# Attention sweep of a hybrid trunk: the value products are divided between the transposes of two heads

## The chip, the cores and the metric

The kernel runs on one NeuronCore of a Trainium2 chip. The metric is the device time of one execution in microseconds (us); the median of three runs of the kernel before is 3368.22 us. The kernel is written by hand in five instruction streams, one for each engine: TensorE (PE, with its weight loads as PEld), VectorE (DVE), ScalarE (ACT), GpSimd (POOL) and SyncE (SP), which wait for one another by semaphores.

## The reference, cut to what matters

One layer over 2048 tokens of width 1024: RMS norm with adaLN, one input projection split in eight, an HGRN2 group of 8 heads, a stick-breaking attention group of 16 heads of size 64, gates, an output projection, a residual and a final norm, all in float32. The change lies in the attention alone:

```python
# one layer: rms norm, adaLN, u = h @ w_in, split in 8; an HGRN2 head group and this one, then w_out
def stick_breaking_attention(q, k, v):     # (1, 2048, 16 heads, 64)
    for nb in range(seq // QBLOCK):        # 128 queries at a time
        z = jnp.einsum('bhtd,bhsd->bhts', qh[:, :, t0:t1], kh[:, :, :t1]) * scale
        mask = jnp.arange(t1)[None, :] < (t0 + jnp.arange(QBLOCK))[:, None]
        log_keep = jnp.where(mask, jax.nn.log_sigmoid(-z), 0.0)
        rc = lax.cumsum(log_keep, axis=3, reverse=True)
        after = jnp.concatenate([rc[..., 1:], jnp.zeros_like(rc[..., :1])], axis=-1)
        w = jnp.where(mask, jnp.exp(jax.nn.log_sigmoid(z) + after), 0.0)
        outs.append(jnp.einsum('bhts,bhsd->bhtd', w, vh[:, :, :t1]))
```

## The kernel before, in words

The functions run one after the other: conditioning and input projection, HGRN2 heads, `stick` (the attention), `output`. Only `stick` is touched.

**The mathematics of `stick`.** With keep = sigmoid(-z), the weights w are differences of the running product `run` of keep from the right. By summation by parts, the output of a query is a sum over keys of (1 - run) times the difference of two neighbouring rows of v. POOL makes these differences (`delta`, tile `ad`, L937). So there are four steps for a piece of a query block: scores z on PE (L966, L969, L971), sigmoid on ACT (L1050, tile `akeep`), running product on DVE (L1086, a tensor_tensor_scan, tile `run`), and then a transposition of each 128x128 block on PE (L983, into `t_ps`), 1 - run on ACT from PSUM (L1058, tile `wt`) and the value product on PE (L1003, into `o_ps`).

**Tiling.** Heads are taken in pairs (e = 0 and 1), and there are 8 pairs. For a pair, the 16 query blocks of 128 are cut into 24 pieces by keys, numbered 0 to 23. Pieces 0 to 7 are query blocks 0 to 7, of 128, 256, ... 1024 keys. Pieces 8 to 15 are blocks 8 to 11, two pieces each: 640, 768, 896 or 1024 keys, and then the first 512. Pieces 16 to 23 are blocks 12 to 15: again 640 to 1024 keys, and then the first 1024. A piece of over 512 keys has two parts (`part_list`), since `t_ps` is two PSUM tiles of 512 columns, used in turn. There are 16 such pieces for a pair of heads (4 to 8, 10, 12, 14 and 16 to 23), and 8 pieces of one part.

**Order of the work.** The order is written out by hand. In step n (of 8 x 24 = 192) PE does `scores` of piece n for both heads, `transposes` of piece n-2 for both heads, `weighted` (the value product) of piece n-3 and, after the last piece of four query blocks, `rows` (L1013: four transpositions of the output back into rows):

```python
if there(n, last):
    scores(i, n)
if there(n - LAG_T, last):
    transposes(i, n - LAG_T)
if there(n - LAG_AV, last):
    weighted(i, n - LAG_AV)
```

ACT goes in the order: output copy of a group (L1038) and squares (L1043) where there are any, the sigmoids of piece n (both heads), the copies `wt` of piece n-2 (head 0, head 1, part after part). DVE does the two scans of piece n. `transposes` waits for the scan of its head (`run_ready`), and from the third part on for the copy of two parts ago (`wt_ready`, because `t_ps` has two tiles). So the first part of head 1 of a two-part piece waits until ACT has copied the first part of head 0. `weighted` waits for the copies of its piece, made one step earlier; in it, each 128 keys are two matmuls of 64 columns, one for each head, in the two halves of the array.

**The tile `run`** has a buffer of 2049 columns for each head and for even and odd query blocks. A row lies at the right end of its buffer, and the last column holds 1, the start of the product. The scan that begins a query block therefore waits until the transpositions of the block two before it are done (`free`).

The 48 steps of two pairs of heads are the body of a hardware loop, which begins at step 7 (`sweep`).

Of the kernel before, what the change touches and what calls it, by code (L numbers as in the profile page):

```python
# [26 lines left out]
P = 128  # L27
D = 1024
SEQ = 2048
KD = D // P  # L30
TB = SEQ // P
# [5 lines left out]
SD = 64  # L37
# [724 lines left out]
def stick(nc, io, keep, scr, o_scr):  # L762
# [15 lines left out]
    NP = len(pieces)  # L778
    PP = 2 * NP
    parts = [[(lo + a, min(512, width - a)) for a in range(0, width, 512)] for _, lo, width in pieces]  # L780
    before = [sum(len(x) for x in parts[:n]) for n in range(NP)]
    NS = sum(len(x) for x in parts)
    group_end = [max(n for n in range(NP) if pieces[n][0] // 4 == g) for g in range(4)]
    half_end = max(n for n in range(NP) if pieces[n][0] < TB // 2)
    SCALE = float(SD) ** -0.5
    NH2 = SH // 2
    with ExitStack() as stack:
        m = Mem(nc, stack)
        q = m.sb("aq", [P, 2, 2, SEQ], F32R)
        k = m.sb("ak", [P, 2, 2, SEQ], F32R)  # L790
        val = m.sb("av", [P, TB, 2 * SD])
        prev = m.sb("ap", [P, TB, 2 * SD])
        delta = m.sb("ad", [P, 2, TB, 2 * SD])
        gat = m.sb("ag", [P, 2, TB, 2 * SD])
        keepf = m.sb("akeep", [P, 2, 2, D])
        run = m.sb("run", [P, 2, 2, SEQ + 1])
        wt = m.sb("wt", [P, 8, 512])
        ot = m.sb("aot", [P, 512])
        og = m.sb("aog", [P, TB, 2 * SD])
# [1 line left out]
        unit_b = m.sb("unit_b", [P, P], BF16)  # L801
        never_b = m.sb("never_b", [P, P], BF16)
        never = m.sb("never", [P, P])
        z_ps = [m.ps(f"z_ps{e}", [P, D]) for e in range(2)]
        t_ps = [m.ps(f"t_ps{a}", [P, 512]) for a in range(2)]
        o_ps = m.ps("o_ps", [P, 512])
# [7 lines left out]
        ones_set = m.sem("ones_set")  # L814
# [16 lines left out]
        def at(n):  # L831

            return (n // NP % 2,) + pieces[n % NP]

        def part_list(n, e):

            base = n // NP * (2 * NS) + 2 * before[n % NP] + e * len(parts[n % NP])
            return [(base + a,) + x for a, x in enumerate(parts[n % NP])]

        def last_part(n, e):  # L840

            return part_list(n, e)[-1][0]

        def group(n):

# [12 lines left out]
        def there(n, last):  # L858
            return 0 <= n and not (last and n >= PP)

        with nc.Block() as block:
# [83 lines left out]
            @block.tensor  # L945
            def _(pe):
                nc.tensor.sem_inc(r_ready, 1)
                pe.wait_ge(ones_set, 3)

                def scores(i, n):  # L950
                    b, qb, lo, width = at(n)
                    if n % NP == 0:
                        pe.wait_ge(k_in[b], i * 64 + 64 * (n // PP + 1))
                        pe.wait_ge(q_in[0], i * 256 + 128 * (n // NP + 1))
                    if n % NP == half_end + 1:
                        pe.wait_ge(q_in[1], i * 256 + 128 * (n // NP + 1))
                    for e in range(2):
                        pe.wait_ge(keep_ready, i * (2 * PP) + (2 * n + e + 1))
                        for a in range(0, width, 512):
                            wd = min(512, width - a)  # L960
                            diag = lo + a + wd == (qb + 1) * P
                            q_hi = q[:, e, 0, qb * P:(qb + 1) * P]
                            q_lo = q[:, e, 1, qb * P:(qb + 1) * P]
                            kk = k[:, b, e, lo + a:lo + a + wd]
                            zz = z_ps[e][:, a:a + wd]
                            nc.tensor.matmul(zz, q_hi, kk, start=True, stop=False)  # L966
                            if diag:

                                nc.tensor.matmul(z_ps[e][:, a + wd - P:a + wd], unit_b[:, :], never_b[:, :],  # L969
                                                 start=False, stop=False, skip_group_check=True)  # L970
                            mm = nc.tensor.matmul(zz, q_lo, kk, start=False, stop=True)  # L971
                        mm.then_inc(z_ready, 1)

                def transposes(i, n):
                    b, qb, lo, width = at(n)
                    for e in range(2):
                        pe.wait_ge(run_ready, i * (2 * PP) + (2 * n + e + 1))
                        src = run[:, e, qb % 2, SEQ - (qb + 1) * P:]
                        for a, key, wd in part_list(n, e):
                            if a >= 2:  # L980
                                pe.wait_ge(wt_ready, i * (4 * NS) + (a - 1))
                            for j in range(wd // P):
                                mm = nc.tensor.transpose(t_ps[a % 2][:, j * P:(j + 1) * P], src[:, key + j * P:key + (j + 1) * P],  # L983
                                                         keep["ident"][:, :])
                            mm.then_inc(t_ready, 1)

                def weighted(i, n):
                    b, qb, lo, width = at(n)
                    diag = lo + width == (qb + 1) * P
                    if diag and qb % 4 == 0:  # L990

                        pe.wait_ge(ot_ready, i * 8 + (4 * (n // NP) + qb // 4 + 1))
                    if n % NP == 0:
                        pe.wait_ge(delta_ready, i * 2 + (n // NP + 1))
                    lists = [part_list(n, e) for e in range(2)]
                    cols = slice((qb % 4) * P, (qb % 4 + 1) * P)
                    for c in range(len(lists[0])):
                        pe.wait_ge(wt_ready, i * (4 * NS) + (lists[1][c][0] + 1))
                        key, wd = lists[0][c][1:]
                        for j in range(wd // P):  # L1000
                            for e in range(2):
                                a = lists[e][c][0]
                                mm = nc.tensor.matmul(o_ps[e * SD:(e + 1) * SD, cols], delta[:, b, key // P + j, e * SD:(e + 1) * SD],  # L1003
                                                      wt[:, a % 8, j * P:(j + 1) * P], start=(diag and key == lo and j == 0),
                                                      stop=(lo == 0 and key + (j + 1) * P == width))
                    mm.then_inc(av_ready, 1)

                def rows(i, n):
                    g = group(n)
                    pe.wait_ge(ot_ready, i * 8 + (g + 2))  # L1010
                    pe.wait_ge(og_ready, i * 8 + (g + 1))
                    for j in range(4):
                        mm = nc.tensor.transpose(r_ps[:, j * P:(j + 1) * P], ot[:, j * P:(j + 1) * P], keep["ident"][:, :])  # L1013
                    mm.then_inc(r_ready, 1)

                def step(i, n, last):
                    if there(n, last):
                        scores(i, n)
                    if there(n - LAG_T, last):
                        transposes(i, n - LAG_T)  # L1020
                    if there(n - LAG_AV, last):
                        weighted(i, n - LAG_AV)
                    if there(n - LAG_R, last) and group(n - LAG_R) is not None:
                        rows(i, n - LAG_R)

                sweep(nc.tensor, step)
# [37 lines left out]
            def _(dve):  # L1064
                nc.vector.sem_inc(red_ready, 1)
                nc.vector.sem_inc(og_ready, 1)
                nc.vector.memset(run[:, :, :, SEQ:SEQ + 1], 1.0).then_inc(ones_set, 1)
                dve.wait_ge(never_in, 16)
                nc.vector.tensor_copy(never_b[:, :], never[:, :]).then_inc(ones_set, 1)
                nc.vector.tensor_copy(unit_b[:, :], keep["ident"][:, :]).then_inc(ones_set, 1)  # L1070
                dve.wait_ge(ones_set, 3)

                def step(i, n, last):
                    if there(n, last):
                        b, qb, lo, width = at(n)
                        diag = lo + width == (qb + 1) * P
                        at0 = SEQ - (qb + 1) * P + lo
                        for e in range(2):
                            dve.wait_ge(keep_ready, i * (2 * PP) + (2 * n + e + 3))
                            if diag and (qb >= 2 or n >= NP):  # L1080

                                free = max(x for x in range(n) if at(x)[1] == (qb - 2) % TB)
                                dve.wait_ge(t_ready, i * (4 * NS) + (last_part(free, e) + 1))
                            if not diag:
                                dve.wait_ge(run_ready, i * (2 * PP) + (2 * (n - 1) + e + 1))
                            nc.vector.tensor_tensor_scan(run[:, e, qb % 2, at0:at0 + width][:, ::-1], keepf[:, e, n % 2, 0:width][:, ::-1],  # L1086
                                                         keepf[:, e, n % 2, 0:width], run[:, e, qb % 2, at0 + width:at0 + width + 1],
                                                         ALU.mult, ALU.bypass).then_inc(run_ready, 1)
                    n2 = n - LAG_OG
                    if there(n2, last) and group(n2) is not None:  # L1090
# [362 lines left out]
```

## Time and profile before

| | us |
|---|---|
| median of 3 runs (range) | 3368.22 (3367.56 to 3371.39) |
| the profiled execution's own time | 3368.85 |
| its span, first to last instruction | 3367.1 |
| PE busy in the span | 3097.2 |
| DVE busy | 1517.6 |
| ACT busy | 973.4 |
| POOL busy | 491.8 |
| mean granted clock of TensorE, share of full | 0.979 |

The profile comes from one execution. A matmul's duration in it runs until its result is out, so matmuls overlap and a PE that shows as busy need not be at its peak; what counts for PE is the distance from one start to the next. In brackets behind a row of the timeline stands the idle time of that engine before the row, and what ended it. "issue" is idle time in which the engine waited for nothing that the profile shows.

### The profile page before, as it was taken

The page shows a single profiled execution, that of the slowest core. Times are in us where ns is not written, and L with a number is a line of the kernel's source. Part 1 is how long each engine was busy: PE and PEld are TensorE (multiplying, and loading weights), DVE is VectorE, ACT ScalarE, POOL GpSimd, SP SyncE. Part 2 cuts the span into 40 slices and gives each one's busy share as a digit, 9 for nine tenths or more (in the row PEclk, how much of TensorE's full clock was granted, in tenths as well). Part 3 has the DMA queues.
Part 4 walks back from the last instruction along what each step waited for, and adds up shares of the span by engine and source line. Part 5 has one row for each costly group of instructions (what it writes and reads, how often), then busy time and mean ns, then how long its engine had stood idle before and what let it go on. Part 6 is the DMA issues. An engine that isn't in the chain of part 4 may idle for free. (4 is left out here: it accounts for less than half of the span.)

```text
span 3367.1 us, 56899 instructions
## 1 busy us (share of the span) xinstructions
PE 3097.2 (92%) x22432; PEld 2721.8 (81%) x22432; DVE 1517.6 (45%) x1652; ACT 973.4 (29%) x1749; POOL 491.8 (15%) x218
## 2 busy tenths in 40 slices
PE   6899999999999999997888859989889998879998
PEld 5788888889999999997888837767767777758887
DVE  5212221111112211225878846866767777654343
ACT  4111111111110111100111136666666666631111
POOL 3211111111111111103545610000000000000000
PEclk9999999999999999998999979999999999989999
DMA  6123334443222122215443192352352351053221
GB/s 271 60 72 99 115 119 123 119 124 100 72 69 72 58 70 72 69 59 195 134 131 112 29 224 51 77 127 51 76 127 52 76 126 39 1 181 118 82 100 38
DMA packets 217944, 327.14 MB, mean 97 GB/s; under 512 B 11680, under 2 KB 159520, under 8 KB 204960
## 3 DMA queue, kind: packets, MB, share of 16 engines
q1 hardware_dynamic: 217296, 324.08, 32.3%
q8 instruction: 114, 1.87, 0.2%
q14 instruction: 70, 0.57, 0.1%
q10 hardware_dynamic: 464, 0.63, 0.1%
HBM read 207.22 MB, written 117.44 MB: 96 GB/s over the span
## 5 line engine op out<-in xcount | busy, mean ns | idle before, releaser
L1086 DVE TENSOR_TENSOR_SCAN run<-akeep,run 128x1024 f32<-128x1024 f32 (+7 forms) x384 | 667.7, 1780 | 286.8 <-ACT akeep L1050 189.1
L983 PE MATMUL t_ps<-ident,run 128*128 128x128 f32 x2176 | 300.8, 278 | 89.5 <-ACT wt L1058 89.5
L1050 ACT ACTIVATE akeep<-z_ps 128x1024 f32<-128x1024 f32 (+7 forms) x384 | 290.9, 776 | 274.4 <-PE z_ps L971 270.1
L983 PEld LDWEIGHTS t_ps<-ident,run 128*128 128x128 f32 x2176 | 243.7, 141 | 134.2 <-ACT wt L1058 87.8
L1058 ACT ACTIVATE wt<-t_ps 128x512 f32<-128x512 f32 (+3 forms) x640 | 306.5, 534 | 55.5 <-PE t_ps L983 54.9
L966 PE MATMUL z_ps<-ak,aq 128*128 128x512 f32 (+3 forms) x640 | 254.4, 397 | 39.9 <-DMA aq<-s_qlo 33.9
L370 PE MATMUL u_ps<-w_hi,h_lo 128*128 128x256 f32 x2048 | 287.5, 283 | 0.0
L370 PE MATMUL u_ps<-w_lo,h_hi 128*128 128x256 f32 x2048 | 287.5, 283 | 0.0
L370 PE MATMUL u_ps<-w_hi,h_hi 128*128 128x256 f32 x2048 | 287.5, 283 | 0.0
L1003 PE MATMUL o_ps<-wt,ad 128*64 128x128 f32 x4352 | 280.5, 277 | 5.6 <-issue 5.6
L643 PE MATMUL hps<-hq,hk 128*128 128x128 f32 x1792 | 219.9, 286 | 50.0 <-DVE hq L733 13.3
L1003 PEld LDWEIGHTS o_ps<-wt,ad 128*64 128x64 f32 x4352 | 234.1, 137 | 37.8 <-issue 37.5
L370 PEld LDWEIGHTS u_ps<-w_hi,h_hi 128*128 128x128 f32 x2048 | 264.3, 192 | 0.1
L370 PEld LDWEIGHTS u_ps<-w_lo,h_hi 128*128 128x128 f32 x2048 | 264.2, 192 | 0.0
L370 PEld LDWEIGHTS u_ps<-w_hi,h_lo 128*128 128x128 f32 x2048 | 264.2, 192 | 0.0
L361 PE MATMUL u_ps<-h_hi,w_hi 128*128 128x512 f32 x1024 | 254.7, 391 | 5.9 <-DVE w_lo L413 5.9
L643 PEld LDWEIGHTS hps<-hq,hk 128*128 128x128 f32 x1792 | 215.1, 201 | 54.6 <-issue 52.4
L361 PE MATMUL u_ps<-h_lo,w_hi 128*128 128x512 f32 x1024 | 253.1, 389 | 0.0
L361 PE MATMUL u_ps<-h_hi,w_lo 128*128 128x512 f32 x1024 | 252.9, 389 | 0.0
L971 PE MATMUL z_ps<-ak,aq 128*128 128x512 f32 (+3 forms) x640 | 252.6, 399 | 0.0
L361 PEld LDWEIGHTS u_ps<-h_hi,w_hi 128*128 128x128 f32 x1024 | 193.2, 189 | 46.5 <-issue 6.3
L340 POOL CAST w_hi<-w_raw 128x2048 fp32r<-128x2048 f32 x31 | 58.8, 1895 | 1163.5 <-DMA w_raw<-in_w_in 1163.5
(140 smaller groups left out, 3621.6 us busy)
## 6 DMA issues: line engine op xcount, KB each, us to landing
w_raw<-in_w_in SPq DMA_DIRECT2D x32, 1024.0 KB, 5.6
aq<-s_qhi SPq DMA_DIRECT2D x64, 256.0 KB, 6.4
aq<-s_qlo SPq DMA_DIRECT2D x64, 256.0 KB, 6.9
o<-s_o SPq DMA_DIRECT2D x16, 1024.0 KB, 6.1
ada<-in_w_ada SPq DMA_DIRECT2D x9, 1024.0 KB, 8.4
xg<-in_x SPq DMA_DIRECT2D x4, 2048.0 KB, 11.0
s_gq<-st SPq DMA_DIRECT2D x32, 256.0 KB
s_gf<-st SPq DMA_DIRECT2D x32, 256.0 KB
```

The lines of the kernel that those rows point to most:

```text
L340: nc.gpsimd.tensor_copy(w_hi[:, par], w_raw[:, :, :]).then_inc(w_split, 1)
L361: mm = nc.tensor.matmul(u_ps[j][:, :], wt[:, par, k, cg * P:(cg + 1) * P], ht[:, k, tp * 512:(tp + 1) * 512], start=(n == 0), stop=(n == 3 ...
L370: mm = nc.tensor.matmul(u_ps[j][:, b * WC:(b + 1) * WC], ht[:, k, tb * P:(tb + 1) * P], wt[:, par, k, :], start=(n == 0), stop=(n == 3 * K ...
L643: mm = nc.tensor.matmul(out, k[:, e, toks], q[:, 2 * u + e, toks], start=True, stop=True)
L966: nc.tensor.matmul(zz, q_hi, kk, start=True, stop=False)
L971: mm = nc.tensor.matmul(zz, q_lo, kk, start=False, stop=True)
L983: mm = nc.tensor.transpose(t_ps[a % 2][:, j * P:(j + 1) * P], src[:, key + j * P:key + (j + 1) * P], keep["ident"][:, :])
L1003: mm = nc.tensor.matmul(o_ps[e * SD:(e + 1) * SD, cols], delta[:, b, key // P + j, e * SD:(e + 1) * SD], wt[:, a % 8, j * P:(j + 1) * P], ...
L1050: nc.scalar.activation(keepf[:, e, n % 2, 0:width], z_ps[e][:, 0:width], ACT.Sigmoid, scale=-SCALE).then_inc(keep_ready, 1)
L1058: nc.scalar.activation(wt[:, a % 8, 0:wd], t_ps[a % 2][:, 0:wd], ACT.Identity, scale=-1.0, bias=1.0).then_inc(wt_ready, 1)
L1086: nc.vector.tensor_tensor_scan(run[:, e, qb % 2, at0:at0 + width][:, ::-1], keepf[:, e, n % 2, 0:width][:, ::-1], keepf[:, e, n % 2, 0:wid ...
```

## The change

`scores`, `transposes` and `weighted` become functions of one head or one part. A step now goes: scores of both heads; transposes of head 0; `weighted` for the first part (up to 512 keys) of piece n-3; transposes of head 1; `weighted` for the second part, where there is one; `rows`. `av_ready` is raised after the last part. The waits themselves are the same.

`run` loses its column of ones; the scan that begins a query block starts from the constant 1.0. Query blocks 0 to 7 lie in halves of 1024 columns (`home`), in turn: among the even blocks, 0 and 4 take the one half and 2 and 6 the other, and the odd ones likewise. The wait `free` then goes back four blocks for blocks 4 to 7, two blocks for blocks 8 and up, and none is needed for blocks 2 and 3 of the first pair of heads.

```diff
@@ -793,7 +793,7 @@
         delta = m.sb("ad", [P, 2, TB, 2 * SD])
         gat = m.sb("ag", [P, 2, TB, 2 * SD])
         keepf = m.sb("akeep", [P, 2, 2, D])
-        run = m.sb("run", [P, 2, 2, SEQ + 1])
+        run = m.sb("run", [P, 2, 2, SEQ])
         wt = m.sb("wt", [P, 8, 512])
...
@@ -841,6 +841,10 @@
 
             return part_list(n, e)[-1][0]
 
+        def home(qb):
+
+            return qb // 2 % 2 * D if qb < TB // 2 else 0
+
...
-                pe.wait_ge(ones_set, 3)
-
-                def scores(i, n):
+                pe.wait_ge(ones_set, 2)
+
+                def scores(i, n, e):
                     b, qb, lo, width = at(n)
-                    if n % NP == 0:
+                    if e == 0 and n % NP == 0:
                         pe.wait_ge(k_in[b], i * 64 + 64 * (n // PP + 1))
                         pe.wait_ge(q_in[0], i * 256 + 128 * (n // NP + 1))
-                    if n % NP == half_end + 1:
+                    if e == 0 and n % NP == half_end + 1:
                         pe.wait_ge(q_in[1], i * 256 + 128 * (n // NP + 1))
...
+                        nc.tensor.matmul(zz, q_hi, kk, start=True, stop=False)
+                        if diag:
+
+                            nc.tensor.matmul(z_ps[e][:, a + wd - P:a + wd], unit_b[:, :], never_b[:, :],
+                                             start=False, stop=False, skip_group_check=True)
+                        mm = nc.tensor.matmul(zz, q_lo, kk, start=False, stop=True)
+                    mm.then_inc(z_ready, 1)
+
+                def transposes(i, n, e):
+                    qb = at(n)[1]
+                    pe.wait_ge(run_ready, i * (2 * PP) + (2 * n + e + 1))
+                    src = run[:, e, qb % 2, home(qb):]
+                    for a, key, wd in part_list(n, e):
+                        if a >= 2:
+                            pe.wait_ge(wt_ready, i * (4 * NS) + (a - 1))
+                        for j in range(wd // P):
+                            mm = nc.tensor.transpose(t_ps[a % 2][:, j * P:(j + 1) * P], src[:, key + j * P:key + (j + 1) * P],
+                                                     keep["ident"][:, :])
+                        mm.then_inc(t_ready, 1)
+
+                def weighted(i, n, c):
                     b, qb, lo, width = at(n)
                     diag = lo + width == (qb + 1) * P
-                    if diag and qb % 4 == 0:
+                    lists = [part_list(n, e) for e in range(2)]
+                    if c >= len(lists[0]):
+                        return
+                    if c == 0 and diag and qb % 4 == 0:
 
                         pe.wait_ge(ot_ready, i * 8 + (4 * (n // NP) + qb // 4 + 1))
-                    if n % NP == 0:
+                    if c == 0 and n % NP == 0:
                         pe.wait_ge(delta_ready, i * 2 + (n // NP + 1))
-                    lists = [part_list(n, e) for e in range(2)]
                     cols = slice((qb % 4) * P, (qb % 4 + 1) * P)
-                    for c in range(len(lists[0])):
-                        pe.wait_ge(wt_ready, i * (4 * NS) + (lists[1][c][0] + 1))
-                        key, wd = lists[0][c][1:]
-                        for j in range(wd // P):
-                            for e in range(2):
-                                a = lists[e][c][0]
-                                mm = nc.tensor.matmul(o_ps[e * SD:(e + 1) * SD, cols], delta[:, b, key // P + j, e * SD:(e + 1) * SD],
-                                                      wt[:, a % 8, j * P:(j + 1) * P], start=(diag and key == lo and j == 0),
-                                                      stop=(lo == 0 and key + (j + 1) * P == width))
-                    mm.then_inc(av_ready, 1)
+                    pe.wait_ge(wt_ready, i * (4 * NS) + (lists[1][c][0] + 1))
+                    key, wd = lists[0][c][1:]
+                    for j in range(wd // P):
+                        for e in range(2):
+                            a = lists[e][c][0]
+                            mm = nc.tensor.matmul(o_ps[e * SD:(e + 1) * SD, cols], delta[:, b, key // P + j, e * SD:(e + 1) * SD],
+                                                  wt[:, a % 8, j * P:(j + 1) * P], start=(diag and key == lo and j == 0),
+                                                  stop=(lo == 0 and key + (j + 1) * P == width))
+                    if c == len(lists[0]) - 1:
+                        mm.then_inc(av_ready, 1)
...
                 def step(i, n, last):
-                    if there(n, last):
-                        scores(i, n)
-                    if there(n - LAG_T, last):
-                        transposes(i, n - LAG_T)
-                    if there(n - LAG_AV, last):
-                        weighted(i, n - LAG_AV)
+                    for e in range(2):
+                        if there(n, last):
+                            scores(i, n, e)
+                    for e in range(2):
+                        if there(n - LAG_T, last):
+                            transposes(i, n - LAG_T, e)
+                        if there(n - LAG_AV, last):
+                            weighted(i, n - LAG_AV, e)
                     if there(n - LAG_R, last) and group(n - LAG_R) is not None:
                         rows(i, n - LAG_R)
...
-                nc.vector.memset(run[:, :, :, SEQ:SEQ + 1], 1.0).then_inc(ones_set, 1)
                 dve.wait_ge(never_in, 16)
                 nc.vector.tensor_copy(never_b[:, :], never[:, :]).then_inc(ones_set, 1)
                 nc.vector.tensor_copy(unit_b[:, :], keep["ident"][:, :]).then_inc(ones_set, 1)
-                dve.wait_ge(ones_set, 3)
+                dve.wait_ge(ones_set, 2)
 
                 def step(i, n, last):
                     if there(n, last):
                         b, qb, lo, width = at(n)
                         diag = lo + width == (qb + 1) * P
-                        at0 = SEQ - (qb + 1) * P + lo
+                        at0 = home(qb) + lo
                         for e in range(2):
                             dve.wait_ge(keep_ready, i * (2 * PP) + (2 * n + e + 3))
-                            if diag and (qb >= 2 or n >= NP):
-
-                                free = max(x for x in range(n) if at(x)[1] == (qb - 2) % TB)
+                            if diag and (qb >= 4 or n >= NP):
+
+                                last_user = TB - 2 + qb % 2 if qb < 4 else qb - 4 if qb < TB // 2 else qb - 2
+                                free = max(x for x in range(n) if at(x)[1] == last_user)
                                 dve.wait_ge(t_ready, i * (4 * NS) + (last_part(free, e) + 1))
                             if not diag:
                                 dve.wait_ge(run_ready, i * (2 * PP) + (2 * (n - 1) + e + 1))
                             nc.vector.tensor_tensor_scan(run[:, e, qb % 2, at0:at0 + width][:, ::-1], keepf[:, e, n % 2, 0:width][:, ::-1],
-                                                         keepf[:, e, n % 2, 0:width], run[:, e, qb % 2, at0 + width:at0 + width + 1],
+                                                         keepf[:, e, n % 2, 0:width],
+                                                         1.0 if diag else run[:, e, qb % 2, at0 + width:at0 + width + 1],
                                                          ALU.mult, ALU.bypass).then_inc(run_ready, 1)
```

## Rows read from the trace of the kernel before

**Rows 1.** The page: TensorE's granted clock over 40 slices, tenths of full.

```profile
PEclk9999999999999999998999979999999999989999
```

**Rows 2.** Windows, the sweep and a later stretch: span, busy time (instructions) by engine, clock, DMA.

```profile
1968.00:2950.00 982.00, 880.16 (x8188) 705.49 (x8188) 703.14 (x446) 614.29 (x1087) 38.61 (x8) 0.99 0.35 81
...
2239.50:2243.00 3.50, 3.30 (x10) 2.04 (x11) 0.00 (x0) 1.02 (x1) 0.00 (x0) 0.60 0.82 226
```

**Rows 3.** Groups by form: line, engine, tiles, shapes xcount | busy us, mean ns | idle before.

```profile
L983 PE MATMUL t_ps<-ident,run 128*128 128x128 f32 x2176 | 300.8, 278 | 89.5 <-ACT wt L1058 89.5
L1003 PE MATMUL o_ps<-wt,ad 128*64 128x128 f32 x4352 | 280.5, 277 | 5.6 <-issue 5.6
L1086 DVE TENSOR_TENSOR_SCAN run<-akeep,run 128x1024 f32<-128x1024 f32 x112 | 257.3, 2338 | 108.1 <-ACT akeep L1050 94.0 <-PE t_ps L983 14.1
L1058 ACT ACTIVATE wt<-t_ps 128x512 f32<-128x512 f32 x448 | 251.0, 599 | 55.3 <-PE t_ps L983 54.9
L983 PEld LDWEIGHTS t_ps<-ident,run 128*128 128x128 f32 x2176 | 243.7, 141 | 134.2 <-ACT wt L1058 87.8 <-issue 30.3 <-DVE run L1086 1.7
```

**Rows 4.** Waits: who waited for whom, us in total, times, longest.

```profile
DVE run L1086 <- PE t_ps L983: 96.6, 58, 5.2
PE t_ps L983 <- ACT wt L1058: 89.5, 128, 1.0
```

**Rows 5.** Timeline of PE, steps 17, 18, 19: start, duration, line, count [idle before].

```profile
2168.70 1.04 PE L983 MATMUL t_ps<-ident,run 128*128 128x128 f32 x8
2169.66 1.97 PE L1003 MATMUL o_ps<-wt,ad 128*64 128x128 f32 x32
2171.56 0.50 PE L966 MATMUL z_ps<-ak,aq 128*128 128x512 f32 x1
...
2173.33 0.71 PE L983 MATMUL t_ps<-ident,run 128*128 128x128 f32 x5
2174.88 0.77 PE L983 MATMUL t_ps<-ident,run 128*128 128x128 f32 x5 [0.84 <-ACT wt L1058]
2175.58 1.09 PE L1003 MATMUL o_ps<-wt,ad 128*64 128x128 f32 x16
2176.60 0.50 PE L966 MATMUL z_ps<-ak,aq 128*128 128x512 f32 x1
```

**Rows 6.** Timeline of PE, end of step 12: value products, `rows`, the next scores.

```profile
2147.11 1.09 PE L1003 MATMUL o_ps<-wt,ad 128*64 128x128 f32 x16
2148.14 0.66 PE L1013 MATMUL r_ps<-ident,aot 128*128 128x128 f32 x4
2148.55 0.48 PE L966 MATMUL z_ps<-ak,aq 128*128 128x512 f32 x1
```

**Rows 7.** Timeline of ACT, steps 18 and 19.

```profile
2172.70 1.64 ACT L1050 ACTIVATE akeep<-z_ps 128x768 f32<-128x768 f32 x2 [1.81 <-PE z_ps L971]
2174.24 0.76 ACT L1058 ACTIVATE wt<-t_ps 128x512 f32<-128x512 f32 x2
2175.57 0.77 ACT L1058 ACTIVATE wt<-t_ps 128x512 f32<-128x512 f32 x2 [0.58 <-PE t_ps L983]
2176.72 0.60 ACT L1038 ACTIVATE aot<-o_ps 128x512 f32<-128x512 f32 x1 [0.38 <-PE o_ps L1003]
2177.83 1.95 ACT L1050 ACTIVATE akeep<-z_ps 128x1024 f32<-128x1024 f32 x2 [0.52 <-PE z_ps L971]
```

**Rows 8.** Timeline of PE: head 1's transposes in steps 6, 8, 9, 19, 24.

```profile
2114.80 0.77 PE L983 MATMUL t_ps<-ident,run 128*128 128x128 f32 x5 [0.95 <-ACT wt L1058]
...
2125.58 0.98 PE L983 MATMUL t_ps<-ident,run 128*128 128x128 f32 x7 [0.50 <-ACT wt L1058]
...
2130.76 1.15 PE L983 MATMUL t_ps<-ident,run 128*128 128x128 f32 x8 [0.35 <-ACT wt L1058]
...
2180.32 1.14 PE L983 MATMUL t_ps<-ident,run 128*128 128x128 f32 x8 [0.73 <-ACT wt L1058]
...
2210.87 1.15 PE L983 MATMUL t_ps<-ident,run 128*128 128x128 f32 x8 [0.25 <-ACT wt L1058]
```

More of the change, by code:

```diff
@@ L956, in scores @@
                         pe.wait_ge(q_in[1], i * 256 + 128 * (n // NP + 1))
-                    for e in range(2):
[L958 to L981, printed above, removed]
-                            for j in range(wd // P):
-                                mm = nc.tensor.transpose(t_ps[a % 2][:, j * P:(j + 1) * P], src[:, key + j * P:key + (j + 1) * P],
-                                                         keep["ident"][:, :])
-                            mm.then_inc(t_ready, 1)
@@ L987, in weighted @@
-                def weighted(i, n):
+                    pe.wait_ge(keep_ready, i * (2 * PP) + (2 * n + e + 1))
+                    for a in range(0, width, 512):
+                        wd = min(512, width - a)
+                        diag = lo + a + wd == (qb + 1) * P
+                        q_hi = q[:, e, 0, qb * P:(qb + 1) * P]
+                        q_lo = q[:, e, 1, qb * P:(qb + 1) * P]
+                        kk = k[:, b, e, lo + a:lo + a + wd]
+                        zz = z_ps[e][:, a:a + wd]
+                        nc.tensor.matmul(zz, q_hi, kk, start=True, stop=False)
[3 more added lines that the diff above has]
+                        mm = nc.tensor.matmul(zz, q_lo, kk, start=False, stop=True)
@@ L994, in weighted @@
                         pe.wait_ge(delta_ready, i * 2 + (n // NP + 1))
-                    lists = [part_list(n, e) for e in range(2)]
                     cols = slice((qb % 4) * P, (qb % 4 + 1) * P)
-                    for c in range(len(lists[0])):
-                        pe.wait_ge(wt_ready, i * (4 * NS) + (lists[1][c][0] + 1))
-                        key, wd = lists[0][c][1:]
-                        for j in range(wd // P):
-                            for e in range(2):
-                                a = lists[e][c][0]
-                                mm = nc.tensor.matmul(o_ps[e * SD:(e + 1) * SD, cols], delta[:, b, key // P + j, e * SD:(e + 1) * SD],
-                                                      wt[:, a % 8, j * P:(j + 1) * P], start=(diag and key == lo and j == 0),
-                                                      stop=(lo == 0 and key + (j + 1) * P == width))
```

## The prediction, made before the changed kernel was seen

> **What bounds the kernel now.** I read the slices first: TensorE's clock is full nearly everywhere, with dips at the joints of stages [rows 1]. Then the windows: the sweep lasts 982 us, PE is busy for 880 of them, DVE for 703, ACT for 614 [rows 2]. So PE bounds the sweep, with about 100 us of gaps. The groups name them: the transposes sat idle for 89.5 us before they could start, always for ACT's copies `wt` [rows 3], in 128 waits of 0.70 us on average and 1.0 at most [rows 4]. 128 is 16 for each of the 8 pairs of heads, which is the number of pieces with two parts: once in each such piece, head 1's transposes wait. DVE's waits for the transposes (96.6 us) [rows 4] cost PE nothing, for PE waited on scans for 1.7 us in all [rows 3]. The timeline shows one wait: in step 18 head 0's five transposes start at 2173.33, head 1's at 2174.88 [rows 5]. What ends last is ACT's chain: the sigmoids start at 2172.70, when head 0's scores are out, and end at 2174.34 by their duration; the copy that starts at 2174.24 is the one that head 1 waits for [rows 7] (0.6 us for 512 columns [rows 3]). The chain hangs on this step's own scores, not on what PE does meanwhile. Work put between the two transposes is therefore free until ACT's copy is done.
>
> **The change, part by part.** First the prices of PE's runs, start to start. Eight transposes and the turn to the value products take 0.96 us (2168.70 to 2169.66) [rows 5]; with 0.109 us a transpose this leaves 0.09 for the turn. The 0.109 comes from the same rows: the copies of two 512-wide tiles apart, a run of x transposes shows 0.27 + (x-1) times 0.109 (five: 0.71, eight: 1.03 to 1.04) [rows 5]. Value products: 32 take 1.90 us until the scores start, 16 take 1.02 [rows 5]. So each costs 0.055, and the turn away from them 0.14. The turn to transposes of `rows` costs the same (16 products: 1.03) [rows 6].
>
> 1. Value products between the heads. The first part is eight matmuls (fewer for blocks 0 to 2). Between head 0 and head 1 they take 0.09 + 0.44 + 0.14 = 0.67 us. The old idle time counts from the end of the last transpose, 0.27 after its start, where the next could have started after 0.11, so the slot is the idle row plus 0.16. The visit is hidden wherever the row shows 0.51 or more; below that it pushes head 1 back by the rest. I call this the overhang.
>
> 2. What is saved behind head 1. Where the piece of the value products has two parts, the later visit remains and is shorter by 0.44. Where it has one part, the later visit goes altogether (0.67), and scores come straight behind transposes; four transposes of `rows` and that turn take 0.41 [rows 6], which is 0.03 less than 4 times 0.109, so I count 0.71.
>
> 3. The 24 steps of a pair, by transposed piece (step n does piece n-2) and value piece (n-3), with the idle rows of one pair [rows 5, 8]; what isn't shown repeats these numbers:
> - two-part transposes, two-part values, idle 0.50 to 0.95 (steps 7, 8, 10, 19 to 23): 8 x 0.44 = 3.5 us
> - two-part transposes, one-part values, idle 0.84 to 0.95 (steps 6, 12, 14, 18): 4 x 0.71 = 2.8
> - short slots: steps 24 and 25 (idle 0.25, overhang 0.26) save 0.18 each; step 9 (0.35, overhang 0.16) 0.28; step 16 (like it, one-part values) 0.55: 1.2
> - one-part transposes, two-part values (steps 11, 13, 15, 17, 26): nothing to hide in, 0.44 - 0.67 = -0.23 each: -1.2
> - one-part transposes, one-part values (steps 3, 4, 5): 0.71 - 0.67, about 0.1 together
>
> That is 6.5 us a pair, 52 for eight pairs.
>
> 4. Is ACT free when the next scores come earlier? In step 18, the tightest, the last copies end at 2176.34, and the output copy then waited for PE's last value product (0.38 idle) [rows 7]. This product now lies earlier, so the output copy runs at 2176.34 to 2176.94. The next sigmoid moves from 2177.83 to 2177.12. That fits by 0.2 us. Elsewhere ACT idles 1.8 us ahead of its sigmoids [rows 7]. In total it has 368 us of idle time in the sweep [rows 2]. I count nothing, at worst 0.35 in the five steps that follow one-part values in a two-part step, 40 x 0.35 = 14 us.
>
> 5. Scans from a constant, and no memset: DVE has 279 us spare [rows 2]. Without this cover a saved or lost 0.1 us on each of 256 first scans would be 26 us of DVE's time. Price on the path: 0, from -1.7 (all that PE waited for scans) to +2.
>
> 6. Halves of `run`: the first scan of blocks 2 to 7 no longer waits for transposes of the same step. This shortens DVE's 96.6 us of waits. On the path it is worth 0 to 1.7 us, since a piece's transposes come two steps after its scan. It is also cover for part 1: head 1's transposes now end up to 0.67 later in one-part steps, and a scan behind them would have too. The longest scans take 2.34 us for a head [rows 3] against two steps of some 5 us each [rows 5].
>
> 7. Order of waits. Ahead of the first value part PE waits for copies that ACT made a whole step earlier. Behind that wait stand head 1's transposes, and ACT's copies behind them. SP's and POOL's queues wait on the scores and the last value product as before, and these come earlier. The loop's turn-round is untouched; the half-clock stretch behind one (0.60 granted over 3.5 us at 2239.5) [rows 2] costs under 2 us and may come or go.
>
> Sum: the profiled execution's own 3368.85 - 52 = 3316.9; it lies 0.6 above the median, so about 3316.
>
> Bounds. If the turns in the middle were free, the eight one-part steps of a pair gain 0.23 each and the four short slots 0.78 together (no more than their overhangs), 21 us in all: 3296. If each of the two turns cost 0.1 more, these 12 x 8 = 96 steps lose 0.2 each, and step 8 nearly as much: 21 us, 3337. If transposes to scores cost as much as values to scores (0.23 more in 64 steps): 15 us, 3331. I take the rows' prices, because both turns are shown dozens of times at the same value.
>
> The Trainium skill speaks against the order of the change: TensorEngine Tiling, Tiling Modes, says "Changing tiling mode (not just tile) drains the TensorE", and the transposes use the whole array while the value products use halves. The trace agrees that a turn costs something, but less than a drain of the matmul's 0.27 us would.
>
> **The rivals.**
> A. The turn drains the array. Each turn in the middle lasts from the last start to its end, 0.27 instead of 0.20 us (0.109 + 0.09), so 0.14 more a visit: 96 x 0.14 = 13 us and 1 for step 8. The time is 3331. Against it: no turn in the rows is that long. For it: no row has a turn from value products to transposes of `run` in mid-sweep. Transposes to scores without a saving gives the same 3331, and I count it here.
> B. Slower: the middle visit itself costs too much. It stands in all 192 steps, in 64 of them in a slot that had no idle time. The point from which it decides is 0.21 more for a turn (0.41 instead of 0.20): 96 steps lose 0.42 each (40 us), and the long slots overflow by 13. At 0.25 more the loss is 48 + 20 = 68 us, so 52 - 68 = -16 and the time 3384. For it: 64 steps pay for a visit that hides nothing. Against it: every turn in the rows.
> C. The wait only moves: ACT's copy comes later by what PE gains, because ACT becomes the bound. Then the 128 waits keep their idle time, the 0.44 to 0.71 is lost, and the one-part steps still pay: 3368 + 8 = 3376 at worst, about 3368 if half. Against it: ACT's 1.8 us of idle time ahead of its sigmoids and the clear chain in step 18.
> D. The halves do what the visits don't: DVE's waits vanish and PE gains by more than 1.7 us. Nothing speaks for it; with everything else it would be 3305 or less.
>
> **How the numbers follow.** This kernel's runs can tell about 0.2% (7 us) from no change. Main case 0.72 (3316, own range 3305 to 3326), A 0.14 (3331), ACT late in part (step 4 above, 3330 to 3345) 0.05, C 0.03, B 0.03, D 0.03. Faster is the main case, A, D and the partly late ACT, less a little: 0.92. Slower is B and part of C: 0.04. Same: 0.04. The range goes from the free turns to ACT late beside A's drain: 3296 to 3341.
>
> **What would show it.** In the profile after, PE's idle time for `wt` should fall from 89.5 us to about 25 (of idle rows of 0.84 stay 0.33 us of waiting, of 0.95 0.44, of 0.73 0.22, together 28 us, of which the rows show 0.07 less each). The start of head 1's transposes, counted from this step's scores, should not move in the steps with 0.84. Each visit of eight products should last 0.58 to the next transpose. One-part steps should be longer by 0.23. DVE's waits for transposes should drop below 50 us with no effect on PE. The forecast is wrong if a turn in the middle measures over 0.3, if ACT's idle time ahead of its sigmoids is used up, or if anything outside the sweep's 982 us changes by over 3 us.

## The result, and the profile after

The changed kernel takes 3287.97 us (median of 4 runs, 3285.98 to 3289.28) against 3368.61 (median of 4) before: a ratio of 0.9759, 95% interval 0.9742 to 0.9776. The gain is 80.6 us, where 52 were forecast, and the time lies below the stated range. The direction and the place were right, the size was not.

The page after has a span of 3286.3 us. These two groups of its fifth part answer to the first two of [rows 3] (busy us, mean ns | idle before):

```profile
L1006 PE MATMUL o_ps<-wt,ad 128*64 128x128 f32 x4352 | 308.1, 280 | 5.5 <-issue 5.5
L985 PE MATMUL t_ps<-ident,run 128*128 128x128 f32 x2176 | 311.8, 278 | 0.1
```

The transposes' idle time for the copies is gone: 89.5 us [rows 3], now 0.1. I had forecast that about 25 would stay. The window of the sweep, to be read beside [rows 2] (span, then busy time of PE, PEld, DVE, ACT, POOL, clock, DMA share, GB/s):

```profile
1969.00:2869.00 900.00, 885.96 (x8192) 701.08 (x8192) 687.42 (x446) 616.42 (x1088) 43.62 (x8) 0.99 0.38 89
```

From the first scores to the end of the last value product the sweep went from 981.3 to 897.3 us, which is 84 us less. The span is 81 us shorter, so the rest of the program is 3 us longer, half of it ahead of the sweep and half behind. The whole gain lies in the sweep. The waits (who for whom, us in total, times, longest):

```profile
ACT akeep L1056 <- PE z_ps L974: 144.0, 145, 31.2
...
DVE run L1092 <- PE t_ps L985: 47.9, 24, 4.9
...
PEld t_ps L985 <- ACT wt L1064: 14.6, 84, 0.2
...
PEld t_ps L985 <- DVE run L1092: 0.3, 2, 0.2
```

And the timeline of PE in steps 17 and 18, which answers to [rows 5]:

```profile
2152.33 0.60 PE L985 MATMUL t_ps<-ident,run 128*128 128x128 f32 x4
2152.85 1.09 PE L1006 MATMUL o_ps<-wt,ad 128*64 128x128 f32 x16
2153.88 0.66 PE L985 MATMUL t_ps<-ident,run 128*128 128x128 f32 x4
2154.47 1.09 PE L1006 MATMUL o_ps<-wt,ad 128*64 128x128 f32 x16
2155.49 0.50 PE L969 MATMUL z_ps<-ak,aq 128*128 128x512 f32 x1
...
2157.25 0.71 PE L985 MATMUL t_ps<-ident,run 128*128 128x128 f32 x5
2157.89 1.09 PE L1006 MATMUL o_ps<-wt,ad 128*64 128x128 f32 x16
2158.92 0.76 PE L985 MATMUL t_ps<-ident,run 128*128 128x128 f32 x5
2159.44 0.48 PE L969 MATMUL z_ps<-ak,aq 128*128 128x512 f32 x1
```

Here the error is to be seen. A visit to the value products (so I call what PE does of them between the transposes of the two heads) is 16 matmuls, 1.03 us to the next transpose; I had priced 8 and 0.58. The first part is 512 keys, 4 blocks for 2 heads, which is 8 calls in the source. The profile counts two matmuls for each call, as the group of before shows (4352 for 8 pairs x 136 blocks x 2 heads = 2176 calls, where the transposes are 2176 for as many calls). In step 18 of before, the piece of 512 keys stood in my own row as x16 [rows 5].

So in step 18 head 0 to head 1 now takes 1.67 us (2157.25 to 2158.92) instead of 1.55 [rows 5]: the visit overfills the slot by 0.12. Behind head 1 the scores come after 0.52 instead of 1.72 us. From head 0's first transpose to the next scores that is 2.19 us instead of 3.27, so 1.08 less, where I had 0.71. In step 17, which had no slot, the time from the first transpose to the next scores went from 2.86 [rows 5] to 3.16: 0.30 longer, where I had 0.23. The difference is the second run of transposes, 0.59 for four instead of 0.52.

ACT in steps 18 and 19, to be read beside [rows 7]:

```profile
2156.62 1.64 ACT L1056 ACTIVATE akeep<-z_ps 128x768 f32<-128x768 f32 x2 [1.45 <-PE z_ps L974]
2158.16 0.76 ACT L1064 ACTIVATE wt<-t_ps 128x512 f32<-128x512 f32 x2
2159.61 0.77 ACT L1064 ACTIVATE wt<-t_ps 128x512 f32<-128x512 f32 x2 [0.69 <-PE t_ps L985]
2160.26 0.61 ACT L1044 ACTIVATE aot<-o_ps 128x512 f32<-128x512 f32 x1
2160.74 1.96 ACT L1056 ACTIVATE akeep<-z_ps 128x1024 f32<-128x1024 f32 x2
```

The copy that head 1 waits for still begins 1.54 us behind the sigmoids (2156.62 to 2158.16; before 2172.70 to 2174.24). The chain did not move against its own scores. As forecast, the output copy now follows the piece copies at once. ACT no longer rests before the sigmoids of step 19, and they begin 1.30 us behind their scores (2159.44 to 2160.74) instead of 1.23. This is not one spot alone: over the sweep ACT's waits for scores fell from 270.1 us (173 times) to 144.0 (145 times), and before 43 of the 192 steps' sigmoids it has no idle time left, where it was 16. But in no kind of step are the sigmoids more than 0.1 us later behind their scores.

### The profile page after: what moved, and what is told of

It reads as the page before. It is cut to its first block and busy times, and to the rows that moved or that the text cites. A ratio compares the mean times of both kernels' runs of the same rounds, so it can differ in the third digit from the quotient of the medians.

```text
span 3286.3 us, 56906 instructions
## 1 busy us (share of the span) xinstructions
PE 3110.6 (95%) x22432; PEld 2724.4 (83%) x22432; DVE 1502.1 (46%) x1651; ACT 975.2 (30%) x1749; POOL 496.8 (15%) x218
## 5 line engine op out<-in xcount | busy, mean ns | idle before, releaser
L1092 DVE TENSOR_TENSOR_SCAN run<-akeep 128x768 f32<-128x768 f32 (+7 forms) x256 | 425.5, 1698 | 172.2 <-ACT akeep L1056 122.3
L1064 ACT ACTIVATE wt<-t_ps 128x512 f32<-128x512 f32 (+3 forms) x640 | 314.1, 536 | 129.7 <-PE t_ps L985 128.7
L1056 ACT ACTIVATE akeep<-z_ps 128x1024 f32<-128x1024 f32 (+7 forms) x384 | 291.1, 778 | 155.6 <-PE z_ps L974 144.0
L1006 PE MATMUL o_ps<-wt,ad 128*64 128x128 f32 x4352 | 308.1, 280 | 5.5 <-issue 5.5
L985 PE MATMUL t_ps<-ident,run 128*128 128x128 f32 x2176 | 311.8, 278 | 0.1
L1092 DVE TENSOR_TENSOR_SCAN run<-akeep,run 128x1024 f32<-128x1024 f32 (+1 forms) x128 | 228.4, 1826 | 47.8 <-ACT akeep L1056 47.8
```

Source lines behind the costliest of these rows:

```text
L1056: nc.scalar.activation(keepf[:, e, n % 2, 0:width], z_ps[e][:, 0:width], ACT.Sigmoid, scale=-SCALE).then_inc(keep_ready, 1)
L1064: nc.scalar.activation(wt[:, a % 8, 0:wd], t_ps[a % 2][:, 0:wd], ACT.Identity, scale=-1.0, bias=1.0).then_inc(wt_ready, 1)
```

## The experiments

All ran beside the kernel before, which took 3371.5 us (median of 13) with the first four and 3370.4 (median of 9) with the last two, so the ratios are what is to be compared.

**The new order of PE alone.** The changed kernel with the tile `run` put back, its column of ones and the scan's start from it included:

```diff
-        run = m.sb("run", [P, 2, 2, SEQ])
+        run = m.sb("run", [P, 2, 2, SEQ + 1])
...
-            return qb // 2 % 2 * D if qb < TB // 2 else 0
+            return SEQ - (qb + 1) * P
...
-                            if diag and (qb >= 4 or n >= NP):
+                            if diag and (qb >= 2 or n >= NP):
```

> The new order of PE's work alone; the tile run as before the change (2049 columns, a column of ones, the scan's wait for the query block two before). Theory 1 (the slots): the whole gain is transposes' slots filled, and the forecast was short because a first part is 16 matmuls in the profile, 0.88 us, where I counted 8. Then this kernel is as fast as the changed one, 3288 +- 4 us. Theory 2 (the halves): the order gives the forecast 52 us, and the rest of the 81 comes from scans that start earlier. Then 3316.

Measured: 3288.24 us, ratio 0.9757 (0.9741 to 0.9774), the same as the whole change. The theory of the slots stands; the halves account for nothing measurable. DVE waits longer for transposes than with the halves, and PE hardly waits for DVE (ACT waits for scans for 7.1 us, with the halves for 7.9):

```profile
DVE run L1092 <- PE t_ps L985: 88.6, 60, 5.8
...
PEld t_ps L985 <- DVE run L1092: 0.2, 1, 0.2
```

**The halves alone.** The changed kernel with PE's order put back:

```diff
                     for e in range(2):
                         if there(n - LAG_T, last):
                             transposes(i, n - LAG_T, e)
+                    for c in range(2):
                         if there(n - LAG_AV, last):
-                            weighted(i, n - LAG_AV, e)
+                            weighted(i, n - LAG_AV, c)
```

> The halves of run and the constant start of the scan alone, with PE's order as before the change. Theory 1: 3368 +- 3 us, DVE's waits for transposes fall by about half (96.6 to 50 us) and PE's wait for the copies stays at 89.5. Theory 2: 3340.

Measured: 3370.67 us, ratio 0.9995 (0.9985 to 1.0005). No effect, though DVE's waits fell by half from the 96.6 us of [rows 4]:

```profile
PE t_ps L985 <- ACT wt L1065: 89.7, 128, 1.0
...
DVE run L1093 <- PE t_ps L985: 49.7, 19, 5.3
```

**A visit of the length that I had priced.** 256 keys of the value piece between the heads, the rest behind:

```diff
+                    if there(n - LAG_T, last):
+                        transposes(i, n - LAG_T, 0)
+                    wide = there(n - LAG_AV, last) and at(n - LAG_AV)[3] > 2 * P
+                    if there(n - LAG_AV, last):
+                        weighted(i, n - LAG_AV, 0, (0, 2) if wide else None)
+                    if there(n - LAG_T, last):
+                        transposes(i, n - LAG_T, 1)
+                    if wide:
+                        weighted(i, n - LAG_AV, 0, (2, 4))
+                    if there(n - LAG_AV, last):
+                        weighted(i, n - LAG_AV, 1)
```

> As the changed kernel, but only the first 256 keys of the value piece (8 matmuls in the profile, 0.44 us) stand between the heads; the rest of its first part comes behind head 1. This is the visit that my forecast priced, except that one-part pieces of 384 and 512 keys now need a second visit too. Theory 1, by the forecast's terms: two-part steps save 0.44 (short slots 0.2 to 0.3), one-part steps lose 0.25, 39 us for eight pairs: 3329, and PE's wait for copies stays at 25 to 35 us. Theory 2: the length of the visit is not what matters, 3288 to 3300.

Measured: 3331.7 us, ratio 0.9884 (0.9867 to 0.9900). That is 39.8 us less than the kernel before beside it, where the terms of the forecast gave 39. The interval leaves some 6 us to either side, but step by step the trace says the same: the twelve kinds of step with a long slot are shorter by 0.42 to 0.45 us, where the forecast had 0.44. So the prices of the turns, of a matmul and of the slots were right, and the count was wrong. The wait for copies stays, less of it than the 25 to 35 us expected:

```profile
PE t_ps L985 <- ACT wt L1072: 20.2, 68, 0.5
```

The timeline in step 18 shows visit, rest of the wait and second visit. The eight matmuls take less than the slot, and head 1 begins 1.56 us behind head 0, as before the change (1.55 [rows 5]):

```profile
2167.87 0.71 PE L985 MATMUL t_ps<-ident,run 128*128 128x128 f32 x5
2168.52 0.66 PE L1008 MATMUL o_ps<-wt,ad 128*64 128x128 f32 x8
2169.43 0.77 PE L985 MATMUL t_ps<-ident,run 128*128 128x128 f32 x5 [0.26 <-ACT wt L1072]
2170.12 0.66 PE L1008 MATMUL o_ps<-wt,ad 128*64 128x128 f32 x8
2170.71 0.50 PE L969 MATMUL z_ps<-ak,aq 128*128 128x512 f32 x1
```

**No second visit.** The whole value piece between the heads:

```diff
-                    for e in range(2):
-                        if there(n - LAG_T, last):
-                            transposes(i, n - LAG_T, e)
-                        if there(n - LAG_AV, last):
-                            weighted(i, n - LAG_AV, e)
+                    if there(n - LAG_T, last):
+                        transposes(i, n - LAG_T, 0)
+                    for c in range(2):
+                        if there(n - LAG_AV, last):
+                            weighted(i, n - LAG_AV, c)
+                    if there(n - LAG_T, last):
+                        transposes(i, n - LAG_T, 1)
```

> As the changed kernel, but all of the value piece (up to 32 matmuls, 1.74 us) stands between head 0's and head 1's transposes, and the next scores come straight behind head 1. It takes a visit away in 16 of 24 steps, and its turns: 0.33 us x 128. Theory 1: 42 us less than the changed kernel, 3246. Rival (ScalarE late): the copies of head 1 now end just ahead of the next sigmoids and push them back by 0.35 us in each of the 128 two-part steps, so that nothing is left of it: 3288 or more, with PE waiting for copies again.

Measured: 3252.57 us, ratio 0.9650 (0.9634 to 0.9666). This beats both kernels: 119 us less than before, 36 less than the same order in two visits (beside it, 3288.24). PE's waits for copies are 1.0 us in all, so the rival of a late ScalarE falls. What ScalarE had to spare is going, though: its waits for scores are down to 70.7 us (270.1 before, 144.0 in the changed kernel), before 74 of the 192 steps' sigmoids it has no idle time, and in step 11 they begin 0.5 us later behind their scores. In step 17 first transpose to next scores takes 2.84 us (2147.75 to 2150.59), against 3.16 with two visits:

```profile
2147.75 0.60 PE L985 MATMUL t_ps<-ident,run 128*128 128x128 f32 x4
2148.28 1.97 PE L1006 MATMUL o_ps<-wt,ad 128*64 128x128 f32 x32
2150.17 0.66 PE L985 MATMUL t_ps<-ident,run 128*128 128x128 f32 x4
2150.59 0.48 PE L969 MATMUL z_ps<-ak,aq 128*128 128x512 f32 x1
```

The gain is 6 us short of the 42. By steps the two traces differ by the expected 0.33 (0.31 to 0.38 in each of the 16 kinds), 44 us in all; the two joints, where the loop's body starts over, give 6 of them back. At the first joint PE idles 4.79 us before the scores, 3.20 in the changed kernel (first row its own, second this one's):

```profile
2217.81 0.79 PE L969 MATMUL z_ps<-ak,aq 128*128 128x512 f32 x1 [3.20 <-issue]
```

```profile
2211.74 0.79 PE L969 MATMUL z_ps<-ak,aq 128*128 128x512 f32 x1 [4.79 <-issue]
```

Behind it the granted clock is 0.51 over 7 us, so nearly all of them at the lower level of 1.2 GHz; behind the same joint of the changed kernel it was 0.76 (the seven us from 2217):

```profile
2211.00:2218.00 7.00, 6.25 (x23) 4.32 (x25) 2.67 (x2) 3.16 (x5) 0.00 (x0) 0.51 1.04 272
```

```profile
2217.00:2224.00 7.00, 6.19 (x38) 4.42 (x38) 3.20 (x4) 3.49 (x6) 0.00 (x0) 0.76 0.77 209
```

Counted over the two steps at each joint, this order loses 3.2 us at the first and 2.9 at the second (clock 0.62 against 0.76 over seven us), 6.0 in all. About 2.5 more go in steps 2 to 4, at the start of the sweep. The joints are as long in the last experiment below, which has the same order of PE (9.5 us of idle time in the two, against 6.5 in the changed kernel). Why this order makes them longer, no run tells.

**Visits only where there is a slot.**

```diff
+                    split = len(part_list((n - LAG_T) % NP, 0)) == 2
...
-                        if there(n - LAG_AV, last):
+                        if there(n - LAG_AV, last) and split:
                             weighted(i, n - LAG_AV, e)
+                    if there(n - LAG_AV, last) and not split:
+                        weighted(i, n - LAG_AV, 0)
+                        weighted(i, n - LAG_AV, 1)
```

> As the changed kernel, but in the 8 steps of 24 whose transposed piece has one part, where no transposes waited before, the value products stay behind head 1 as before the change. Theory (a visit without a slot costs its turns): the steps 11, 13, 15, 17 and 26 were longer by 0.25 to 0.31 us in the changed kernel, which is 11 us for eight pairs; steps 3 to 5 are as before. So 11 us less than the changed kernel: 3277 +- 3. If the longer steps came from something else, ScalarE's or VectorE's later start say, part of them stays and the time is between 3282 and 3288.

Measured: 3276.36 us, ratio 0.9722 (0.9709 to 0.9736). Step for step, only the five kinds named are shorter, by 0.29 to 0.31 us each, 11.4 us in all. In step 17 the 2.86 us of before are back:

```profile
2152.38 1.03 PE L985 MATMUL t_ps<-ident,run 128*128 128x128 f32 x8
2153.35 1.97 PE L1006 MATMUL o_ps<-wt,ad 128*64 128x128 f32 x32
2155.24 0.50 PE L969 MATMUL z_ps<-ak,aq 128*128 128x512 f32 x1
```

**All between the heads, with the old `run`.** The edits of the first and the fourth experiment together.

> All value products between the heads, with the tile run as before the change. Theory 1 (the halves do nothing for PE): as e4_all_between, 3252 +- 3 us. Rival (the halves are cover): head 1's transposes now end latest of all orders, a scan of blocks 2 to 8 that waits for them starts up to 1.9 us later, and with steps of only 2.1 to 3.6 us in the short blocks PE comes to wait for scans: 0.5 us in each of 7 steps of 24, 28 us more, 3280.

Measured: 3254.82 us, ratio 0.9658 (0.9644 to 0.9671), against 0.9650 with the halves: no difference that can be told. Even in the order that ends head 1's transposes latest, DVE's waits don't reach PE:

```profile
DVE run L1094 <- PE t_ps L985: 85.8, 60, 6.4
...
PEld t_ps L985 <- DVE run L1094: 0.9, 5, 0.2
```

## Why the prediction was wrong

**What bounds the kernel** was read rightly. Once the wait for the copies was filled (89.5 us of PE's idle time, now 0.1), the time fell by 80.6 us, and all of it in the sweep.

**Step 1, the length of a visit: this failed.** "The first part is eight matmuls": it is sixteen, and "0.09 + 0.44 + 0.14 = 0.67" should have read 0.09 + 0.88 + 0.14 = 1.11. I multiplied a count from the source by a duration per row of the profile, whose rows count two for each call. With 1.11 and everything else as forecast, the sum of step 3 becomes:

- two-part transposes and values: 0.88 in step 7 (no overhang), 0.77 in steps 10, 20, 22 (slot 1.00), 0.66 in steps 19, 21, 23 (slot 0.89), 0.43 in step 8 (slot 0.66): 5.6
- one-part values: 1.15 in step 6, 1.04 in steps 12, 14, 18: 4.3
- short slots and one-part steps as forecast: 0.1 together, since there the time that moves into the middle comes off the end, and only the turns and the slot count

That is 10.0 us a pair and 80 in all, against 80.6 measured. The agreement is a little better than the method: the trace has 10.3 us a pair by steps, and 84 in the whole sweep, and the rest of the program gave 3 back. The same terms with eight matmuls gave 39 for the short visit, against 39.8 measured. Both ends of the forecast's method are thus tested, and the count was the step that failed. The stated bounds all varied prices and ACT; none asked whether the count was right, so the range could not hold it. (Its upper end was also added up short: ACT late and A's drain, 14 and 14 us, lead from 3316 to 3344, not to 3341.)

**Step 2** was right in form: the scores come straight behind the transposes, in 0.52 us for five (5 x 0.109 = 0.55, less the 0.03 of `rows`).

**One-part transposes with two-part values** cost 0.25 to 0.31 each where 0.23 was said, because transposes behind a visit take 0.06 us longer until the next value products (eight take 1.02 in step 9, where the first run takes 0.96). Taking these visits away gave 11 us back. This was the part of the change that costs time.

**Step 4, ACT:** the output copy found its place, and PE's wait for copies is 0.1 us, 1.0 with all value products between. But "ACT idles 1.8 us ahead of its sigmoids" took one row for all: by kind of step it was 0 to 2.4 us before the change. The forecast named the using up of this idle time as a sign of being wrong. It is used up in 43 steps, and this cost PE nothing that shows.

**Steps 5 and 6:** nothing for PE, as forecast. The whole of the order's gain is there without the halves, and the halves alone move nothing. That they are needed as cover also fell, in the order where it was likeliest. The forecast that DVE's waits would fall below 50 us held (47.9).

**Rivals.** A (a turn drains the array for 0.27 us) fell. Turns in mid-sweep look like those in [rows 5, 6]: from the first of sixteen value products to the next transpose is 1.03 us, as from value products to scores before. The Trainium skill (TensorEngine Tiling (Array Packing), Tiling Modes) says that changing the tiling mode drains TensorE; this trace shows 0.09 to 0.1 us above the ordinary spacing for such a change, under the 0.27 us that a matmul takes to its end. B (slower) fell: a visit without a slot cost 0.25 to 0.31 us, at most 0.08 above the 0.23 of the forecast, where B needed 0.42 above it. C (the wait moves) fell with ACT's chain, which moved by 0.1 us at most against its scores. D (3305 or less through the halves) would have named the right side for a wrong reason; the first two experiments exclude it.

## What to carry to other kernels

Take the count and the duration of a run of matmuls from the same row of the profile, never the one from the source: in float32, a call can be two instructions there. When an engine waits for a copy that hangs on the start of its own step, put as much finished work into the wait as there is, also more than fits, for here the surplus cost nothing, since it would have stood behind the wait anyway; what costs is a second visit with its turns. Look then at what the other engine has to spare: here 270 us of ScalarE's waits went to 71. A wait of an engine off the critical path can be halved for no gain at all, as VectorE's was.

## What the runs showed of the hardware

A transposition costs 0.109 us from start to start and one value product's instruction 0.055 on average. These instructions start in pairs, 0.007 us apart, and 0.10 us pass to the next pair; the trace doesn't say which two of the four for 128 keys (two heads, two for each call) make a pair. Changing from the whole array to its halves or back adds about 0.1 us each way: the first start behind a change comes 0.20 us after the last one before it (median of 317 changes one way and of 193 the other in the changed kernel). Between transposes and the next scores, both on the whole array, nothing is added: the scores start 0.03 us behind the last transpose. The scan over 1024 columns that starts from a constant took 2.28 us against 2.34 from a column in memory:

```profile
L1092 DVE TENSOR_TENSOR_SCAN run<-akeep,run 128x1024 f32<-128x1024 f32 x64 | 147.0, 2338 | 41.3 <-ACT akeep L1056 41.3
L1092 DVE TENSOR_TENSOR_SCAN run<-akeep 128x1024 f32<-128x1024 f32 x48 | 107.3, 2278 | 22.4 <-ACT akeep L1056 22.4
```
